# A hybrid decoder trunk on one core: the gated product's residual moves from GpSimd to VectorE

## The reference

```python
def swiglu(h, w_gate, w_up, w_down):
    return (jax.nn.silu(h @ w_gate) * (h @ w_up)) @ w_down

def moe_swiglu(h, router, w_gate, w_up, w_down):
    top_val, top_idx = lax.top_k((h @ router).astype(jnp.float32), TOP_K)   # 2 of 8
    gates = jnp.einsum('btk,btke->bte', jax.nn.softmax(top_val, axis=-1), one_hot(top_idx))
    for e in range(N_EXPERTS):
        out = out + gates[..., e:e + 1] * swiglu(h, w_gate[e], w_up[e], w_down[e])
```

## Time and profile before

| | us |
|---|---|
| median of 3 runs | 3019.67 (3012.88 to 3020.87) |
| profiled execution | 3020.0 |
| its span, first to last instruction | 3017.8 |
| busy PE / DVE / ACT / POOL | 2599.6 / 1691.3 / 1452.7 / 353.8 |
| mean granted TensorE clock | 0.949 of 2.4 GHz |

### The profile page before, as it was taken

The page is one execution under the profiler, slowest core; times in us unless marked ns, Lnnn a source line. Parts: engine busy times, 40 slices in busy tenths (PEclk is TensorE's granted clock), DMA queues, the critical chain, the costliest instruction groups (busy, mean ns, idle before and its releaser), DMA issues.

```text
span 3017.8 us, 67151 instructions
## 1 busy us (share of the span) xinstructions
PE 2599.6 (86%) x29799; PEld 2135.1 (71%) x29818; DVE 1691.3 (56%) x1990; ACT 1452.7 (48%) x1904; POOL 353.8 (12%) x180
## 2 busy tenths in 40 slices
PE   6988888899788989888988997878888888888887
PEld 5766666777466768666756875657787788878876
DVE  2445453234215532545542343149999989999996
ACT  2233343233224321433343323248887878888785
POOL 0000001000000000000010000002322322332231
PEclk9999999999999999899989999989999999999999
DMA  5401030133217634211120232249999999999994
GB/s 183 147 29 57 21 94 29 37 101 105 94 56 256 205 105 136 71 43 30 57 70 23 80 109 84 98 175 385 373 354 363 363 354 368 357 362 365 354 366 183
DMA packets 304032, 531.34 MB, mean 176 GB/s; under 512 B 18528, under 2 KB 145760, under 8 KB 303360
## 3 DMA queue, kind: packets, MB, share of 16 engines
q1 hardware_dynamic: 303600, 525.99, 50.4%
q10 hardware_dynamic: 144, 1.05, 0.1%
HBM read 524.91 MB, written 2.10 MB: 175 GB/s over the span
## 4 chain that ended last, share of the span: by engine, by line
PE 64%; DVE 16%; ACT 12%; issue 7%; DMA 0%; ACTq 0%; POOL 0%; DVEq 0%; SPq 0%
PE bank L797 11%; PE bank L698 9%; DVE arena L2680 8%; PE bank L1368 6%; PE bank L1385 4%; PE bank L768 4%; PE bank L1268 4%; PE bank L1227 4%; ACT arena L1989 4%; PE bank L763 3%; PE bank L716 2%; PE bank L642 2%; PE bank L1412 2%; PE bank L1284 2%; DVE yacc L2688 2%
## 5 line engine op out<-in xcount | busy, mean ns | idle before, releaser
L2680 DVE TENSOR_TENSOR arena<-ring,arena 128x2048 bf16<-128x2048 f32 x336 | 813.9, 2441 | 81.9 <-ACT arena L1989 81.9
L1989 ACT ACTIVATE arena<-ring 128x2048 bf16<-128x2048 f32 x336 | 630.4, 1907 | 0.0
L1368 PE MATMUL bank<-arena 128*128 128x0 bf16 x10752 | 489.0, 209 | 42.8 <-DVE arena L2680 32.6
L1368 PEld LDWEIGHTS bank<-arena 128*128 128x128 bf16 x10752 | 478.7, 99 | 49.0 <-DVE arena L2680 35.7
L797 PE MATMUL bank<-feat,ring 128*128 128x256 f32 x1664 | 436.6, 401 | 8.4 <-ACT ring L1554 2.3
L1518 POOL TENSOR_TENSOR arena<-yacc,arena 128x512 bf16<-128x512 f32 x112 | 296.5, 2647 | 1060.2 <-ACT arena L2012 1060.2
L797 PEld LDWEIGHTS bank<-feat,ring 128*128 128x128 f32 x1664 | 310.0, 197 | 88.2 <-issue 43.5
L1385 PEld LDWEIGHTS bank<-arena 128*128 128x128 bf16 x5376 | 254.9, 102 | 15.8 <-issue 10.5
L1385 PE MATMUL bank<-arena 128*128 128x0 bf16 x5376 | 260.2, 212 | 1.2 <-DVE arena L2680 1.1
L698 PE MATMUL bank<-feat,ring 128*128 128x256 f32 x1056 | 230.7, 381 | 5.8 <-issue 5.8
L698 PEld LDWEIGHTS bank<-feat,ring 128*128 128x128 f32 x1056 | 201.6, 191 | 34.7 <-issue 7.1
(11 more groups left out here) (353 smaller groups left out, 3382.1 us busy)
## 6 DMA issues: line engine op xcount, KB each, us to landing
ring<-in_moe_w_gate SPq DMA_DIRECT2D x112, 1024.0 KB, 7.0
ring<-in_moe_w_up SPq DMA_DIRECT2D x112, 1024.0 KB, 6.5
ring<-in_moe_w_down SPq DMA_DIRECT2D x112, 1024.0 KB, 7.0
ring<-in_w_in SPq DMA_DIRECT2D x76, 1024.0 KB, 5.2
ring<-in_xa_w_kv SPq DMA_DIRECT2D x16, 1024.0 KB, 5.4
ring<-in_ffn_w_gate SPq DMA_DIRECT2D x11, 1024.0 KB, 5.3
ring<-in_ffn_w_up SPq DMA_DIRECT2D x11, 1024.0 KB, 5.4
ring<-in_ffn_w_down SPq DMA_DIRECT2D x11, 1024.0 KB, 6.9
```

Source lines behind the costliest of these rows:

```text
L1368: m = mm(o, w[k // 4][wi][:, k % 4, col:col + P], xg[:, e % 2, xi, k, :].shape_from_register(width[e % 2]), start=i == 0 and k == 0, stop= ...
L1989: sc.activation(w_parts[b][0], ring[:, b * FFN_SLOT:(b + 1) * FFN_SLOT], ACT.Copy).then_inc(S["w_hi"], 1)
L2680: v.tensor_tensor(w_parts[b][1], ring[:, b * FFN_SLOT:(b + 1) * FFN_SLOT], w_parts[b][0], ALU.subtract).then_inc(S["w_lo"], 1)
```

## The change

The residual of the gated product is made on VectorE, and GpSimd's loop in the expert stage is gone. The residual of pair 2n stands behind the low part that follows product(2n), and that of pair 2n + 1 behind the first low part that follows product(2n + 1). VectorE waits for mo_ah, the high part made by ScalarE, before each. The operands, types and the semaphore that it raises stay as they were.

```diff
-            for q in range(2 * NE * STEPS):
-                pool.wait_ge(S["mo_ah"], q + 1)
-                pair = slice(2 * (q % 4), 2 * (q % 4) + 2)
-                nc.gpsimd.tensor_tensor(act_parts[1][:, pair, :], sil[:, q % 4], act_parts[0][:, pair, :], ALU.subtract
-                                        ).then_inc(S["mo_al"], 1)
...
+                def residual_of(q):
+
+                    dve.wait_ge(S["mo_ah"], q + 1)
+                    pair = slice(2 * (q % 4), 2 * (q % 4) + 2)
+                    v.tensor_tensor(act_parts[1][:, pair, :], sil[:, q % 4], act_parts[0][:, pair, :], ALU.subtract).then_inc(S["mo_al"], 1)
...
                     product(2 * n)
                     if more:
                         lo()
+                    residual_of(2 * n)
                     product(2 * n + 1)
                     side(n, 1)
                     if more:
                         lo()
+                    residual_of(2 * n + 1)
+                    if more:
                         lo()
                     side(n, 2)
```

## The result

| | before | after |
|---|---|---|
| median | 3020.05 us (3012.88 to 3020.87, 4 runs) | 3066.19 us (3063.92 to 3068.93, 4 runs) |
| profiled execution's span | 3017.8 | 3066.3 |
| busy DVE / ACT / POOL | 1691.3 / 1452.7 / 353.8 | 1707.4 / 1451.9 / 57.9 |
| mean granted TensorE clock | 0.949 | 0.943 |

The ratio is 1.0156, with a 95% interval of 1.0144 to 1.0168: the kernel is 46 us slower. The forecast was 3059, with a range of 3040 to 3070.

A forecast was written before the change was run, and what follows sets the result against it. It took a ring of waits between VectorE, ScalarE and TensorE to bound most steps, VectorE's load some of the first and last experts': 3020.0 + 26.0 for steps + 13.5 for clock falls = 3059.5, stated as 3059 us, range 3040 to 3070.

The forecast's parts named there:

- every such gap falls: Rival: TensorE's clock drops to 1.2 GHz after all four long gaps of a middle expert; 3070 us, chance 0.08.
- The ring: Expert stage: VectorE, ScalarE and TensorE wait on each other in a loop; a late second product delays the next step equally.
- the first residual: VectorE, between a low part and the second product: +0.60 us in each of steps f = 1 to 6 of later experts.
- The second residual lies in room: VectorE, behind the low part after the second product: the residual of 2n+1 fits by about 0.2 us.
- Steps of f = 0 at +0.12, load-bound ones at -0.14: An expert's first step: +0.60 less 0.48 of GpSimd's hold-up; first-expert steps where VectorE never stops: 1.20 added, 1.34 back.
- Sum of the step prices, +26.0: Whole expert stage: first expert +1.2, six middle experts +22.3, last +2.2, the very end about +0.3 us.
- The clock, +13.5: TensorE: longer gaps bring 9 more drops to 1.2 GHz, at 1.5 us each.
- a gap of 3.1 us is near an edge: TensorE waiting for the second product: gaps of like length fall or don't; 3.7 us is on the bad side.
- The rival in which load alone decides: VectorE's load decides everywhere: hold-up costs 1.34 a step, both residuals 1.20; -8 us, 3012 us, chance 0.03.
- The rival of the transfers: DMA transfers set the pace in the expert stage and the added time disappears in theirs; 3020 us, chance 0.04.
- as many falls as before: Rival: TensorE's clock falls as often as before, leaving only the step prices; 3046 us, chance 0.20.
- GpSimd's hold-up, 52.4 us, mostly worth nothing: VectorE's low parts, lengthened by GpSimd's residuals: 52.4 us all goes, but mostly where low parts have room and buys nothing.

The follow-up runs named there:

- e10: Changed kernel with TensorE's gaps filled by 20 unused matmuls, plus one more same-shape subtraction on VectorE ahead of the residual of pair 2n: 3082.31 us.
- e1: Changed kernel with the residual of pair 2n moved behind the second product and its side work, both residuals still on VectorE: 3026.57 us, ratio 1.0028.
- e4: Kernel before, with VectorE making only the residual of pair 2n, at its place in the changed kernel; GpSimd keeps the other: 3072.66 us.
- e5: Kernel before, with VectorE making only the residual of pair 2n + 1, at its place in the changed kernel; GpSimd keeps the other: 3023.86 us.
- e9: Kernel before with TensorE's gaps filled, GpSimd's residual cut to 4 of 256 columns from the third step on: 2993.30 us.
- the filled kernels: Changed kernel and kernel before, each with 20 unused matmuls in each of four TensorE gaps per middle expert: 3026.56 us and 3003.89 us.
- e3: Kernel before with 20 unused matmuls added in TensorE's gaps of steps f = 1, 2, 4, 5: 3003.89 us, ratio 0.9956.
- e11: Changed kernel with the two products next to each other on VectorE and their high parts next to each other on ScalarE: 2974.82 us.
- the off-ring kernels: Changed kernel with both residuals behind the second product, without and with 20 unused matmuls in TensorE's gaps: 3026.57 us and 2999.35 us.

## Why the prediction was right, and by how much

The steps came out as forecast. The clock did not: what happened is the rival *every such gap falls* (3070, given 0.08), and not the forecast's 9 falls. The range held because it let that rival in.

*The ring was the bound, and the first residual costs 0.60 a step.* Right. The slot is 0.60, and the steps with no change of the clock are longer by 0.60 (f = 1: 16.99 to 17.59; f = 4: 17.65 to 18.25). e10 added 0.60 a step again; e1 and e4 show that the place costs and not the work.

*The second residual lies in room.* Right, and to the tenth: I gave 0.2 us to spare, and the low part behind it waits 0.18. e5 adds only that residual and is 0.2% slower than before, with a clock that fell oftener.

*Steps of f = 0 at +0.12, load-bound ones at -0.14.* Measured +0.13 and -0.14. e9 shows the credit apart: 0.48 in a step of f = 0.

*Sum of the step prices, +26.0.* In the profiles the stage from n = 0's first product to n = 55's second grew by 47.4 us. Of that, 14 new falls (below) are 14 x 1.62 = 22.7, and the falls that were there already got cheaper by about 1 (against the filled kernels the fall at f = 2 cost 1.46 before and 1.36 after, that at f = 5 1.62 and 1.56); so 25.7 are the steps'. The filled pair has 3.74 an expert for 3.72.

*The clock, +13.5.* The direction was right, and the price nearly (the 1.7 read from two neighbouring steps is 1.62 against e3, since these steps differ by 0.08 without a fall, and the fall at f = 2 costs less); the number of falls was not. This is the term that was mis-sized: I took 9 more falls and there were 14 on the ring: two in each of six middle experts (f = 3 grew by 2.24 and f = 6 by 2.20, so 1.64 and 1.60 beside their 0.60), one in the first expert and one in the last. I had taken 1.25 of the two gaps a middle expert that did not yet fall; both did, in every expert. So the term is 22.7 less 1 where I had 13.5, or 8 us more, and the stage grew by 47.4 us for 39.5. The remaining 1 us of the profiled difference arose ahead of the stage.

The reason that I gave for some falls, that a gap of 3.1 us is near an edge and one of 3.7 beyond it, is not borne out as it stands. Gaps of 3.75, 3.70 and 3.78 us did each bring a fall, but the length of the gap does not decide alone. At n = 22 a gap of 2.61 us had a slow stretch behind it before, and one of 3.21 us at the same place had none after; in e10 gaps of 2.1 to 2.4 did. First before, with the window of the slow stretch, then after:

```profile
2399.74 0.63 PE L642 MATMUL bank<-cs,arena 128*128 128x128 f32 x4 [2.61 <-ACT arena L2021]
2400.21 5.84 PE L1368 MATMUL bank<-arena 128*128 128x0 bf16 x96
...
2411.58 1.11 PE L642 MATMUL bank<-cs,arena 128*128 128x128 f32 x4 [3.04 <-ACT feat L2030]
```

```profile
2401.00:2404.40 3.40, 3.40 (x48) 3.40 (x45) 2.62 (x2) 3.40 (x4) 0.00 (x0) 0.51 1.04 333
```

```profile
2417.47 0.63 PE L642 MATMUL bank<-cs,arena 128*128 128x128 f32 x4 [3.21 <-ACT arena L2015]
2417.93 4.24 PE L1368 MATMUL bank<-arena 128*128 128x0 bf16 x96
...
2429.91 1.12 PE L642 MATMUL bank<-cs,arena 128*128 128x128 f32 x4 [5.24 <-ACT feat L2024]
```

The same rows show when a fall is free. The 96 matmuls took 5.84 us slow and 4.24 fast, but the gap behind them was 3.04 and is now 5.24, which is those 1.60 and the 0.60 of the residual: the slow stretch was paid out of a gap, and the step f = 1 is 16.99 with it and 16.99 to 17.00 without (the last three middle experts of e1).

*The rival in which load alone decides* was wrong for this order and right for the next: in e11 VectorE is 97% busy, and who makes the residual is then decided by load. The rival of the transfers is out for these two kernels: no high part waits in either, and e11 runs the transfers at 371 GB/s. They are not far off, though: high parts wait for them in e9's first expert, and for 5.5 us in all in e11. The rival of "as many falls as before" missed by 20 us.

*GpSimd's hold-up, 52.4 us, mostly worth nothing.* Right: 49 came back in VectorE's busy time. In the time, the step prices of the change hold (+0.13 and -0.14, with the residual's 0.60 and 1.20 in them); with no residual in its place, by e9, some 5 us.

What stays open: why the clock falls at one gap and not at another of the same or a greater length, and why some executions of the filled and the off-ring kernels had extra slow stretches early in the stage. No run here isolates that.

## What to carry to other kernels

Ask of an added instruction where it stands between two hand-overs to other engines, and only then what it weighs: 67 us of work, half of it in the wrong slot, cost 46 us, and the same work with that half behind the second product cost 7 with the clock's part in it and nothing without. The same question finds gains: the low part between the two products was on that ring too, and moving it as well gave 52 us more (e1 to e11). Look at TensorE's gaps together with its clock, since a delay of 0.6 us brought 1.6 more with it here, and ask of a slow stretch whether a gap behind it takes it up; and when the bound changes, ask again which engine should do a thing.

## What the runs showed that I had not expected

The falls of the clock are not scattered. Before, they sit at the same three places of each of the six middle experts (at 2401.0, 2411.3 and 2465.9 in the fourth expert; the first is the free one), and after at the same four (2429.4, 2449.9, 2487.4 and 2507.9), all on the ring, so that six experts in a row take 129.68 to 129.71 us. In e1, which begins with an irregular stretch, the step with the first fall drifts from 18.27 to 18.46 over the experts, and the expert from 122.65 to 122.86, within 0.03 of the length it has before, though its step f = 0 is 0.14 shorter: the pattern settles.

Twenty matmuls with unused results in each of four gaps an expert made the kernel before 0.4% faster, with nothing else changed.

Two subtractions on GpSimd one right behind the other hold VectorE up more (6.04 for 4.48 us, so 1.56) than two that come 2.8 us apart (2.65 and 2.75 for 2.28 each on the ring, so 0.84; 1.34 in the load-bound steps).
